# The feed-forward's joints in a hybrid decoder layer: later transposes, earlier first loads, accumulator loads one by one

## What is computed

```python
x = layer_norm(alpha * x + mix, ln1_g, ln1_b)          # mix: three head groups, one output projection
ff = jnp.square(jax.nn.relu(x @ w_ff1)) @ w_ff2        # w_ff1 1024 x 4096, w_ff2 4096 x 1024
x = layer_norm(alpha * x + ff, ln2_g, ln2_b)
```

## Time and profile before

| | |
|---|---|
| three runs, us | 2282.78, 2287.63, 2288.93 (median 2287.63) |
| the profiled execution, us | 2285.08 |
| its span, first to last instruction, us | 2283.4 |
| mean granted TensorE clock | 0.980 of full |
| TensorE busy with matmuls | 2152.9 us, 94% of the span |
| VectorE, ScalarE, GpSimd busy | 1395.9, 1012.4, 595.4 us |
| moved by the DMA engines | 374.06 MB, mean 164 GB/s |

### The profile page before, as it was taken

How to read it: one execution, slowest core, us unless ns; L and a number is a source line. 1 busy time by engine, 2 the same in 40 slices (tenths; PEclk the granted TensorE clock), 3 DMA queues, 4 the chain that set the end, 5 groups by cost and what they waited for, 6 DMA issues and landing times.

```text
span 2283.4 us, 25743 instructions
## 1 busy us (share of the span) xinstructions
PE 2152.9 (94%) x9792; PEld 1735.3 (76%) x9792; DVE 1395.9 (61%) x1871; ACT 1012.4 (44%) x1360; POOL 595.4 (26%) x547
## 2 busy tenths in 40 slices
PE   7999999999899988879999899999799999999995
PEld 5787787778777876758888788888678888778884
DVE  4668565756675675844655677566376544864458
ACT  4534353445344433544544555444333333633334
POOL 3213021202120223220010144444798000620004
PEclk9999999999999999989999999999899999999998
DMA  6222333323232322345464786768866566666653
GB/s 186 56 56 88 97 97 97 93 83 111 83 102 83 122 75 90 93 163 199 155 216 145 255 285 250 276 228 284 322 236 200 193 194 193 211 227 192 195 191 128
DMA packets 241050, 374.06 MB, mean 164 GB/s; under 512 B 16368, under 2 KB 117776, under 8 KB 240928
## 3 DMA queue, kind: packets, MB, share of 16 engines
q1 hardware_dynamic: 212096, 272.68, 36.9%
q0 software_dynamic: 28832, 99.74, 12.3%
HBM read 272.74 MB, written 99.61 MB: 163 GB/s over the span
## 4 chain that ended last, share of the span: by engine, by line
PE 49%; DVE 4%; DMA 3%; issue 3%; ACT 2%; POOL 0%; SPq 0%; ACTq 0%; POOLq 0%; DVEq 0%
PE main L68 8%; PE main L69 8%; PE main L70 8%; PE sc L68 6%; PE sc L69 6%; PE sc L70 6%; DVE w_lo L1574 2%; DMA w_b<-in_w_ff_dram 1%; PE ob L70 1%; PE aux L68 1%; PE ob L68 1%; PE aux L69 1%; PE ob L69 1%; PE aux L70 1%; DMA x_ops<-xop_dram 1%
## 5 line engine op out<-in xcount | busy, mean ns | idle before, releaser
L1574 DVE TENSOR_TENSOR w_lo<-w_b,w_hi 128x1024 fp32r<-128x1024 f32 x144 | 210.9, 1467 | 254.3 <-ACT w_hi L1544 254.3
L1574 DVE TENSOR_TENSOR w_lo<-raw,w_hi 128x1024 fp32r<-128x1024 f32 x144 | 205.3, 1429 | 146.7 <-ACT w_hi L1544 146.7
L1544 ACT ACTIVATE w_hi<-raw 128x1024 fp32r<-128x1024 f32 x144 | 152.3, 1059 | 252.6 <-PE main L70 110.9
L1060 DVE TENSOR_TENSOR w_lo<-raw,w_hi 128x1024 fp32r<-128x1024 f32 x116 | 144.0, 1248 | 164.3 <-ACT w_hi L770 163.1
L1544 ACT ACTIVATE w_hi<-w_b 128x1024 fp32r<-128x1024 f32 x144 | 152.3, 1058 | 183.0 <-PE aux L70 81.1
L68 PE MATMUL main<-xT_lo,w_hi 128*128 128x512 f32 (+1 forms) x528 | 219.6, 416 | 1.5 <-DVE xT_lo L1072 1.5
L70 PE MATMUL main<-xT_hi,w_hi 128*128 128x512 f32 (+1 forms) x528 | 207.9, 394 | 0.0
L69 PE MATMUL main<-xT_hi,w_lo 128*128 128x512 f32 (+1 forms) x528 | 207.5, 393 | 0.0
L770 ACT ACTIVATE w_hi<-raw 128x1024 fp32r<-128x1024 f32 x116 | 122.0, 1054 | 141.7 <-DMA raw<-in_w_in_dram 68.5
L68 PE MATMUL main<-w_lo,w_hi 128*128 128x512 f32 x448 | 175.4, 391 | 9.1 <-DVE w_lo L1574 9.1
L68 PE MATMUL sc<-x_lo,w_hi 128*128 128x512 f32 x448 | 178.7, 399 | 5.3 <-ACT z L1871 2.7
(11 more groups left out here) (257 smaller groups left out, 4921.7 us busy)
## 6 DMA issues: line engine op xcount, KB each, us to landing
raw<-in_w_in_dram SPq DMA_DIRECT2D x80, 512.0 KB, 3.8
h_dram<-z SPq DMA_DIRECT2D x64, 512.0 KB, 4.2
raw<-h_dram SPq DMA_DIRECT2D x112, 256.0 KB, 2.7
w_b<-h_dram SPq DMA_DIRECT2D x112, 256.0 KB, 2.7
h_dram<-h_s SPq DMA_DIRECT2D x48, 512.0 KB, 4.5
rows<-in_x_dram POOLq DMA_DIRECT2D x32, 512.0 KB, 4.9
raw<-in_w_out_dram SPq DMA_DIRECT2D x32, 512.0 KB, 3.7
raw<-in_w_ff_dram SPq DMA_DIRECT2D x32, 512.0 KB, 6.6
```

The costliest lines, as they stand in the source:

```text
L1060: dve.tensor_tensor(w_lo[:, j % RING, :], raw[:, j % RAW, :], w_hi[:, j % RING, :].bitcast(F32), ALU.subtract).then_inc(lo_done, 1)
L1544: act.activation(ff.w_hi[:, n % RING, :], slot_tile(ff, m), ACT.Copy).then_inc(ff.hi_done, 1)
L1574: dve.tensor_tensor(ff.w_lo[:, n % RING, :], slot_tile(ff, m), ff.w_hi[:, n % RING, :].bitcast(F32), ALU.subtract).then_inc(ff.lo_done, 1)
```

## The change

1. Transposition steps 8 and 9 move one place on: step 8 goes to chunk 0 behind o = 4 (where 9 was) and step 9 to chunk 1 behind o = 1. Steps 10 to 15 stay. ACT's and DVE's parts move with them.
2. In the last chunk SP's loads of k = 4..7 are put between the stores.
3. POOL first loads only the two rows of the first normalisation, then `acc[0]` tile by tile, each behind a further use of a ring slot (four tiles, the scaling, four tiles). `acc[1]` is loaded after `init(0)`, a tile every two slots from slot 32 of the contraction, and then the other two rows.

```diff
@@ -1423,6 +1423,10 @@
 TAIL = 4
 
 
+def x_late_step(chunk):
+    return X_STEPS if chunk == 0 else X_STEPS + 1 + chunk
+
+
 def piece_set(q):
     return q % 2 if q < 6 else 0
 
@@ -1669,16 +1673,25 @@
                     sp.wait_ge(h_stored[p], 16 * HALF_CHUNKS)
                 for k in range(4):
                     load(0, 0, k)
+            ahead = chunk == CHUNKS - 1
+            if ahead:
+                load(0, 0, 4)
             sp.wait_ge(h_ready, 4 * chunk + 2)
             store(chunk, 6)
+            if ahead:
+                load(0, 0, 5)
             sp.wait_ge(hs_ready, 4 * chunk + 1)
             store(chunk, 1)
             sp.wait_ge(h_ready, 4 * chunk + 3)
             store(chunk, 0)
+            if ahead:
+                load(0, 0, 6)
             sp.wait_ge(hs_ready, 4 * chunk + 2)
             store(chunk, 2)
             sp.wait_ge(hs_ready, 4 * chunk + 3)
             store(chunk, 4)
+            if ahead:
+                load(0, 0, 7)
         sp.wait_ge(h_ready, 4 * CHUNKS)
         store(CHUNKS - 1, 5)
         sp.wait_ge(hs_ready, 4 * CHUNKS)
@@ -1689,7 +1702,7 @@
                     sp.wait_ge(h_stored[p], 16 * CHUNKS)
             for p in range(PRODUCTS):
                 for k in range(KF):
-                    if hf == 0 and p == 0 and k < 4:
+                    if hf == 0 and p == 0 and k < 8:
                         continue
                     load(hf, p, k)
         for i, c in enumerate(range(TAIL, NT)):
@@ -1738,16 +1751,25 @@
             pool.wait_ge(t_step, 4 * k + 4)
             pool.dma_start(ff.t_dram[3, k, :, :], b21).then_inc(t_stored, 16)
 
+        def load_row(dst, src):
+            pool.dma_start(dst[:, :], src.to_broadcast([P, dst.shape[1]])).then_inc(row_landed, 16)
+
+        def load_acc(hf, c, slots):
+
+            pool.wait_ge(slot_used, EXPAND_SLOTS + slots)
+            pool.dma_start(acc[hf][:, c, :], normed[HALF * hf + P * c:HALF * hf + P * c + P, :]
+                           ).then_inc(acc_landed[hf][c], 16)
+
         pool.wait_ge(slot_used, EXPAND_SLOTS)
-        for dst, src in ((g1_row, ln1_g), (b1_row, ln1_b), (g2_row, ln2_g), (b2_row, ln2_b)):
-            pool.dma_start(dst[:, :], src.to_broadcast([P, dst.shape[1]])).then_inc(row_landed, 16)
-        for hf in range(2):
-            for c in range(NT):
-                pool.dma_start(acc[hf][:, c, :], normed[HALF * hf + P * c:HALF * hf + P * c + P, :]
-                               ).then_inc(acc_landed[hf][c], 16)
-        pool.wait_ge(row_landed, 16 * 4)
+        load_row(g1_row, ln1_g)
+        load_row(b1_row, ln1_b)
+        for c in range(4):
+            load_acc(0, c, 1 + c)
+        pool.wait_ge(row_landed, 16 * 2)
         for row in (g1_row, b1_row):
             pool.tensor_scalar(row[:, :], row[:, :], ALPHA, None, ALU.mult).then_inc(row_scaled, 1)
+        for c in range(4, 8):
+            load_acc(0, c, 2 + c)
         pool.wait_ge(row_scaled, 2)
 
         def init(hf):
@@ -1771,7 +1793,12 @@
                            ).then_inc(out_stored[c], 16)
 
         init(0)
+        for c in range(NT):
+            load_acc(1, c, 2 * KF + 2 * c)
+        load_row(g2_row, ln2_g)
+        load_row(b2_row, ln2_b)
         init(1)
+        pool.wait_ge(row_landed, 16 * 4)
         for c in range(NT):
             finish(0, c)
         for c in range(TAIL):
@@ -1815,10 +1842,10 @@
                                     ff.x_hi[:, kt, X_OF[o], :], ff.x_lo[:, kt, X_OF[o], :],
                                     o in STARTS and kt == 0, kt == 3, onto=o not in STARTS)
                 ins.then_inc(slot_used, 1)
-                if o == 1 and chunk == 0:
-                    x_transposes(pe, ff, X_STEPS)
+                if o == 1 and chunk == 1:
+                    x_transposes(pe, ff, X_STEPS + 1)
                 elif o == 4 and chunk < HALF_CHUNKS - 1:
-                    x_transposes(pe, ff, X_STEPS + 1 + chunk)
+                    x_transposes(pe, ff, x_late_step(chunk))
 
         def piece(hf, p, k, t):
             n = FIRST + EXPAND_SLOTS + CONTRACT_SLOTS * hf + KF * p + k
@@ -1912,8 +1939,8 @@
             snapshot(chunk, 1, b)
             slot_high(act, ff, m + 1)
             back(1)
-            if chunk == 0:
-                x_evacuate(act, ff, X_STEPS)
+            if chunk == 1:
+                x_evacuate(act, ff, X_STEPS + 1)
             snapshot(chunk, 2, a)
             slot_high(act, ff, m + 2)
             back(2)
@@ -1926,7 +1953,7 @@
             slot_high(act, ff, m + 5)
             squared(chunk, 2, z11)
             if chunk < HALF_CHUNKS - 1:
-                x_evacuate(act, ff, X_STEPS + 1 + chunk)
+                x_evacuate(act, ff, x_late_step(chunk))
             back(5)
             act.wait_ge(slot_used, PRODUCTS * chunk + 7)
             if chunk == 0:
@@ -2009,8 +2036,8 @@
             slot_sum(dve, ff, m)
             low(0)
             low(1)
-            if chunk == 0:
-                x_sums(dve, ff, X_STEPS)
+            if chunk == 1:
+                x_sums(dve, ff, X_STEPS + 1)
             low(2)
             completed(chunk, 0, b, z12)
             low(3)
@@ -2028,7 +2055,7 @@
             if m + 6 < EXPAND_SLOTS:
                 slot_sum(dve, ff, m + 6)
             if chunk < HALF_CHUNKS - 1:
-                x_sums(dve, ff, X_STEPS + 1 + chunk)
+                x_sums(dve, ff, x_late_step(chunk))
             dve.wait_ge(h_ready, 4 * chunk + 3)
             dve.wait_ge(hs_ready, 4 * chunk + 1)
             kept(chunk, 2)
```

## The result

| | before | after | after, second time |
|---|---|---|---|
| median, us | 2288.28 | 2262.89 | 2260.47 |
| lowest to highest, runs | 2282.78 to 2291.12, 4 | 2257.16 to 2264.30, 4 | 2258.98 to 2262.34, 4 |
| ratio to before, 95% interval | | 0.9891 [0.9876, 0.9907] | 0.9886 [0.9871, 0.9901] |
| the profiled execution, its span, us | 2285.08, 2283.4 | 2263.95, 2262.2 | 2262.34, 2260.6 |
| granted clock | 0.980 | 0.983 | 0.981 |

The second time stood beside seven runs of the kernel before (median 2286.91). The change is faster by 25.4 us and 26.4 us. All times and ratios here are of fast executions; one of the ten of the transpositions alone took 3052.69 us at a granted clock of 0.654 and is left out. The forecast was a gain of 30.4 us; the time lies inside the range, the gain is 4 to 5 us smaller than the sum.

What follows compares the result with a forecast made beforehand. Two TensorE waits for late transfers were taken as the cost: step 8's `x_piece` and the load of k = 4. Gains 10.7 + 19.7 = 30.4 us took the median from 2287.63 to 2257.2 us, range 2249 to 2268.

Steps and rivals of the forecast that it cites:

- Two joints: Feed-forward: TensorE idles 16.27 us before step 8's transpositions; late loads from k = 4 cost the contraction 22.4 us.
- only the transpositions pay: Rival, chance 0.06: at the contraction the wait moves with the loads, parts 2 and 3 give half, 11 us; 2266.
- step 8's wait back at step 9: Rival, chance 0.05: POOL's chain piece by piece bounds the transpositions, piece 9 late by 5 us; 2262.
- POOL's queue never empty: Slower rival, chance 0.03: gated tiles keep SP's queue at 139 GB/s through product 0 and later; 2294.5.
- Crowding went on: Rival, chance 0.22: POOL's tiles still overlap k = 7..15, nine pieces cost 1.05 us more each; 2264.
- Part 1: Moved transposition steps: idle before o = 2 of chunk 0 falls from 16.3 to 5.3 us; 10.7 us net gain.
- piece 9: Step 9's x piece, needed after o = 1 of chunk 1, lands at 1031.9: new wait 0.3 us, bounds 0 and 1.
- Parts 2 and 3: Contraction's start: early loads of k = 4..7 and spread POOL transfers gain 19.7 of 22.4 us; 2.7 stay.
- The lower bound: Contraction's start: with all rates as from 1622.3 to 1628, k = 8 comes 9.3 us late.
- the sentence on 358 GB/s: By the skill's 358 GB/s instead of 413, k = 8 is 4.9 us late, parts 2 and 3 gain 17.5 us.
- The first four `acc` loads: Beside load k = 8: they take 7.7 us, SP moves 1.07 MB meanwhile, then 1.58 MB alone in 3.8 us.
- POOL's cover: `init(0)` starts at about 1647, four pairs end at 1660 or 1663, before product 0 ends at 1666.1; covered by 3 us.

Runs made afterwards that it cites:

- late execution: First profiled execution of the changed kernel, whose contraction is 7.2 us late at its last pieces; 2263.95 us.
- second series: The changed kernel itself measured once more, with no edit, beside seven runs of the kernel before; median 2260.47 us, ratio 0.9886.
- the late store: Changed kernel with rows and first tiles behind later slot uses, tiles 4 to 7 and step 9 later, and GpSimd's last `t_dram` store delayed by four extra subtractions; 2252.72 us.
- the delayed store: Changed kernel with GpSimd's last `t_dram` store delayed by four extra copies of a subtraction; 2267.09 us.

## Why the prediction was right, and where its sum was too high

**Bottleneck and direction: right.** Two joints, each with one transfer that comes late; both became short, and each part alone gives its own gain. The rivals with less (only the transpositions pay, step 8's wait back at step 9, POOL's queue never empty) did not come. Crowding went on in the mild form of one late load, not of nine pieces at 3.77 us each: behind piece 9 TensorE has no wait.

**Part 1: forecast 10.7, measured 9.6** (B, 67.43 to 57.83). The idle time before o = 2 was to be 5.3 and is 4.95. Half the clock followed at about unchanged length, as said. The mis-sized term is piece 9: "The new wait is 0.3 us, bounded by 0 and by 1 us", and it is 1.43 and 1.57 in the two profiles, 1.47 with the transpositions alone. It was a difference of two times near 1031.8, of which one, the landing, was put together from the load of another piece.

**Parts 2 and 3: forecast 19.7, measured 15.1 in one execution and 21.1 in the other** (D, 22.3 less 7.2 or 1.2), both inside the bounds of 13.1 and 22.4. (The lower bound is added up wrongly by 0.4 us: with the latency and the low part of the forecast, 11.7 and 6.0 us from 1628 on bring piece 8 8.9 us late, not 9.3, and the bound is 13.5; in the same way the 4.9 us of the sentence on 358 GB/s should be 4.4. Neither changes what follows.) In the late execution piece 7 is 2.3 us late where 2.0 was forecast. Piece 8 was to be 2.7 late, and its first matmul starts at 1640.41, 5.4 us behind its due time of 1613.22 + 8 x 2.72 = 1634.98. The step that failed in the late execution is "The first four `acc` loads, 2.10 MB at 274 GB/s, take 7.7 us more [...]; the other 1.58 MB go at 413 GB/s". It let SP's queue run alone to the end of load 8, though the same part of the text has the next tiles issued ahead of `init(0)`. They came at 1630.68 and 1632.77 and moved 0.95 MB in 1634 to 1638; at that stretch's 418 GB/s over both queues these take 2.3 us away from load 8. By this estimate that term alone makes 2.7 into 5.0. The runs bear it out: among the three profiles in which piece 7 is late alike, by 2.3 to 2.4 us, piece 8 is 5.4 and 5.5 us late with these two tiles in place and 3.2 us without them. In the second series the same two tiles are issued as far behind the start, 17.5 and 19.6 us, and piece 8 is only 0.8 us late, less than the forecast: there SP had the load of piece 8 issued 7.6 us behind the start, in the late execution 11.9.

The second thing left out is the clock: behind an idle time of 2.88 us piece 8 took 4.45 us at half clock instead of 2.72, so 1.7 us. The prediction had priced half clock only within the long waits of before.

The third is that the queue's state at the contraction's start was taken as one number. It is not: the bytes that SP's queue moved around it differ by a quarter between executions of the same code, and 6 us of D go with them.

**The aside on bandwidth.** In 1630 to 1634 and 1634 to 1638 the core's transfers ran at 406 and 418 GB/s, nearly all of it between DRAM and SBUF. The Trainium skill (DMA: Bandwidth & Descriptors, section Bandwidth) gives about 358 GB/s per core as what binds transfers between DRAM and SBUF, which is what the prediction quoted, but says beside its measurements that this is each core's share when both cores of the pair stream. Here one core runs, and this case's trace is above 358, after as before. The Trainium skill (Perfetto Trace Analysis, section Roofline) says that a core whose neighbour is idle can pull more and is bounded by its DMA engines at about 435 GB/s; the trace agrees with that, with 418 in those 4 us.

**Shares of the queues.** While both are busy they move like numbers of packets, 142 and 129 in 1616 to 1619, but 0.54 and 0.22 MB, as before the change. The Trainium skill (DMA: Bandwidth & Descriptors, section Queues, rings and completion order) says that a DMA engine takes turns between its queues packet by packet; the trace agrees.

**POOL's cover: right.** `init(0)` was forecast from 1647 in the times of before, which are 6.64 us behind those of after here (1619.86 and 1613.22), so 1640.4. That held 2.7 us of lateness; with 7.1 instead it is 1644.8, and it began at 1645.86. The first `add` did not wait for it.

**The median.** By stretches the change is worth 9.6 + 15.1 = 24.7 or 9.6 + 21.1 = 30.7 us, and the medians say 25.4 and 26.4. The forecast gain of 30.4 fits the better execution only. The first interval, 0.9876 to 0.9907, means a gain of 21.3 to 28.4 us, the second one of 22.6 to 29.5: both leave 30.4 out, by little. The size of the miss, 4 to 5 us, is that of D beyond the forecast in the late execution (7.2 - 2.7 = 4.5), but that this is its cause is not shown. The second series' profile has a D of 1.2 us and is yet the slowest of its four executions, because A and C together are 7.2 us longer than in the profile of before. So the miss can as well lie in A and C, and no other execution of either series was profiled.

## What to carry to other kernels

When a load's way is computed through a shared queue, list every transfer that is issued until it lands, those of the stretch that one has just called free as well: one tile of 0.52 MB beside a load costs, by an estimate from 418 GB/s, 1.3 us, and the waits of 2.88 and 2.22 us here cost another 1.7 and 1.9 at half clock. Transfers that nobody needs for 30 us, here rows and accumulator tiles, belong behind the point where the urgent queue has caught up; moving the rows and the first four tiles behind the third to seventh slot use and the other four behind the fourth pair removed the last wait at no cost that shows, and in all three profiles of such versions, one of them with the late store, D is 0.0. And where parts of a program spread by several microseconds from one execution to the next, compare stretches cut at fixed instructions, and profile the same kernel twice before a theory is built on one reading.

## What was not expected of the hardware

- SP's issue instructions themselves can take microseconds. The load from `h_dram` for piece 8 took 4.20 us to issue in the late execution, against 0.33 us for the same load of piece 7 before it and 0.49 us for that of piece 8 in the second series. What the instruction waits for is not shown. Timeline of SP, after:

```profile
1616.68 0.33 SPq L1646 DMA_DIRECT2D w_b<-h_dram  x1
...
1619.20 4.20 SPq L1646 DMA_DIRECT2D raw<-h_dram  x1
1623.45 1.69 SPq L1656 DMA_DIRECT2D raw<-in_w_ff_dram  x1
```

- In the same stretch behind the issue of the rows, 4.7 to 7.7 us, all queues together ran at 271 GB/s in one profile of the changed kernel and at 388 in another.
- An idle time of 2.88 us at piece 8 was followed by half clock, and so was one of 2.22 us at piece 7 with the delayed store. One of 1.43 us at step 9 was not (the clock is 1.00 in 1026 to 1028), nor one of 2.14 us at piece 7 with tiles 4 to 7 later (1.00 in 1634 to 1638).
